# Rearranging the two MLPs of a two-block transformer kernel: when their staging, modulation and last evacuations are issued

## What is computed

```python
def first_block(x, ...):
    for layer in range(2):
        ...                                        # attention of this layer -> mix
        x = layer_norm(ALPHA * x + mix, ...)
        x = layer_norm(ALPHA * x + sqrelu_mlp(x, mlp_w_up[layer], mlp_w_down[layer]), ...)
    return x                                       # sqrelu_mlp: relu(x @ up)**2 @ down, width 4096

def second_block(x, c, ctx, c_ctx, w_ada, ...):
    sh1, sc1, g1, sh2, sc2, g2 = ada(c, w_ada, b_ada)          # silu(c) @ w_ada + b_ada
    csh1, csc1, ... = ada(c_ctx, w_ada, b_ada)
    u_ctx = (layer_norm_2(ctx) * (1 + csc1) + csh1) @ w_in
    u_lat = (layer_norm_2(x) * (1 + sc1) + sh1) @ w_in
    ...                                            # token mixer, post-norm, convolutional FFN
```

## Time and profile before

| what | value |
|---|---|
| time, three runs | 1914.8, 1915.16, 1920.2 us; median 1915.16 |
| the profiled execution | 1919.75 us, of which the span of the trace is 1918.0 us |
| `mlp0`, `mlp1` in the trace | about 317 to 672 us and 946 to 1300 us |
| PE busy | 96% of the span |
| mean granted clock of TensorE | 0.986 of full speed |

### The profile page before, as it was taken

The page is one execution under the profiler, slowest core; times in us unless marked ns, Lnnn a source line. Parts: engine busy times, 40 slices in busy tenths (PEclk is TensorE's granted clock), DMA queues, the critical chain, the costliest instruction groups (busy, mean ns, idle before and its releaser), DMA issues.

```text
span 1918.0 us, 25530 instructions
## 1 busy us (share of the span) xinstructions
PE 1833.0 (96%) x9436; PEld 1491.5 (78%) x9436; DVE 1390.3 (72%) x2217; ACT 883.0 (46%) x1512; POOL 825.0 (43%) x570
## 2 busy tenths in 40 slices
PE   9999899999989999989999998999999999999997
PEld 7876578878777788866887876778887788888876
DVE  4568857888889752175789897985559788676766
ACT  4247643444356432384243444746444554444342
POOL 1234533554541010183345554415346557676740
PEclk9999999999999999999999999999999999999999
DMA  7331032888765432202288877641211323333344
GB/s 282 114 92 45 1 143 92 326 310 298 271 244 189 146 111 93 105 2 88 89 299 314 301 273 271 209 158 67 88 45 66 110 89 110 112 119 121 111 153 153
DMA packets 67048, 297.86 MB, mean 155 GB/s; under 512 B 9008, under 2 KB 9328, under 8 KB 46576
## 3 DMA queue, kind: packets, MB, share of 16 engines
q1 hardware_dynamic: 59872, 254.45, 38.0%
q0 software_dynamic: 7056, 41.80, 5.8%
HBM read 258.54 MB, written 35.65 MB: 153 GB/s over the span
## 4 chain that ended last, share of the span: by engine, by line
PE 65%; DVE 21%; DMA 6%; ACT 3%; issue 2%; POOL 2%; SPq 0%; ACTq 0%; DVEq 0%; POOLq 0%
PE G L474 29%; PE G L2938 8%; PE G L2869 5%; DMA KS_sb<-ada 4%; PE OB L2938 3%; DVE weights_low L685 2%; PE TR L474 2%; PE OB L474 2%; PE G L1923 2%; DVE w_sb L3415 2%; PE TR L2938 2%; PE G L2888 2%; DVE og_sb L3415 2%; PE TR L2869 1%; PE OB L1923 1%
## 5 line engine op out<-in xcount | busy, mean ns | idle before, releaser
L474 PE MATMUL G<-xt_high,weights_high 128*128 128x512 f32 (+1 forms) x1224 | 451.2, 369 | 2.4 <-issue 1.7
L474 PE MATMUL G<-xt_low,weights_high 128*128 128x512 f32 (+1 forms) x1224 | 449.0, 367 | 0.0
L474 PE MATMUL G<-xt_high,weights_low 128*128 128x512 f32 (+1 forms) x1224 | 448.9, 367 | 0.0
L518 POOL TENSOR_TENSOR weights_low<-ring_sb,weights_high 128x1024 fp32r<-128x1024 f32 (+2 forms) x102 | 246.3, 2427 | 285.3 <-ACT weights_high L512 285.3
L512 ACT ACTIVATE weights_high<-ring_sb 128x1024 fp32r<-128x1024 f32 (+2 forms) x188 | 189.8, 1019 | 158.4 <-PE G L2869 40.0
L474 PEld LDWEIGHTS G<-xt_high,weights_high 128*128 128x128 f32 x1224 | 228.7, 187 | 42.6 <-issue 3.7
L474 PEld LDWEIGHTS G<-xt_high,weights_low 128*128 128x128 f32 x1224 | 228.5, 187 | 38.5
L474 PEld LDWEIGHTS G<-xt_low,weights_high 128*128 128x128 f32 x1224 | 228.8, 187 | 37.9
L518 DVE TENSOR_TENSOR weights_low<-ring_sb,weights_high 128x1024 fp32r<-128x1024 f32 (+1 forms) x86 | 109.5, 1282 | 169.3 <-ACT weights_high L512 169.2
L685 DVE TENSOR_TENSOR weights_low<-ring_sb,weights_high 128x1024 fp32r<-128x1024 f32 x130 | 173.3, 1343 | 58.8 <-ACT weights_high L679 58.3
L679 ACT ACTIVATE weights_high<-ring_sb 128x1024 fp32r<-128x1024 f32 x130 | 136.5, 1052 | 73.9 <-PE OB L2938 40.5
(11 more groups left out here) (631 smaller groups left out, 4321.6 us busy)
## 6 DMA issues: line engine op xcount, KB each, us to landing
...
```

The lines of the kernel that those rows point to most:

```text
L474: mm = nc.tensor.matmul(out, lhsT=a, rhs=b, start=(3 * i + j == 0), stop=(3 * i + j == n - 1))
L518: tt_(out=quarter_part(wl, stage, n), in0=quarter_part(raw_quarter(stage, n), stage, n), in1=quarter_part(wh, stage, n), op=ALU.subtract). ...
```

## The change

It has four parts, in both MLPs.

1. **Modulation steps.** The steps run behind c = 1 to 16 and 18 to 26 with no c left out but 17. The sums, the first turn (behind U17 instead of U18) and the copies move up; the second turn stands behind U30 instead of D14.
2. **Staging first.** DVE makes the low part of the staged block, or the hidden sums, ahead of the copy, the move and the modulation steps of the same c. On both ACT and DVE the blocks of D13 and D14 are staged at the start of c = 30 and c = 31, ahead of the weights split there, and the weights of D15 are split after the loop instead of in c = 31.
3. **Eight raw slots in the last phase.** C's raw weights take eight slots, four of them in the first half of `ring`. S15's split weights go to row 0 instead of row 3. The first chunks of the next stage's weights can be loaded once C9 and C11 are split (before, C13 and C15).
4. **Evacuations.** The seventh product is emptied behind S15 instead of behind C1, the sixth behind C4, C5 and C6, the two half statistics of layer norm behind C7. In `mlp1` `scale_columns` goes from behind C3 to behind C8, and the first half of the context's modulation on ACT from C8 to C9.

```diff
+    C_RAW = [(1, 2), (1, 3), (1, 0), (1, 1), (0, 3), (0, 0), (0, 1), (0, 2)]
...
-    ADA_SUM_BEHIND = {7: 0, 10: 1, 13: 2, 16: 3, 21: 4, 25: 5, 28: 6, 31: 7}
-    ADA_TURN_BEHIND = {18: 0}
-    ADA_STEPS = {1: (0, (0,)), 2: (0, (1, 2)), 3: (0, (3, 4, 5)), 4: (0, (6, 7)), 6: (1, (0, 1, 2)), 7: (1, (3, 4, 5)), 8: (1, (6, 7)),
...
-    ADA_COPY, ADA_MOVE = {18: 0}, {20: 0}
+    ADA_SUM_BEHIND = {6: 0, 9: 1, 12: 2, 15: 3, 19: 4, 22: 5, 25: 6, 28: 7}
+    ADA_TURN_BEHIND = {17: 0, 30: 1}
+    ADA_STEPS = {1: (0, (0,)), 2: (0, (1, 2)), 3: (0, (3, 4, 5)), 4: (0, (6, 7)), 5: (1, (0, 1, 2)), 6: (1, (3, 4, 5)), 7: (1, (6, 7))}
+    for job, c in ((2, 8), (3, 11), (4, 14), (5, 18), (6, 21), (7, 24)):
+        ADA_STEPS.update({c: (job, (0, 1, 2)), c + 1: (job, (3, 4, 5)), c + 2: (job, (6, 7))})
+    ADA_COPY, ADA_MOVE = {17: 0, 30: 1}, {18: 0, 31: 1}
...
             if kind == "S":
-                return [x[:, 3, 512 * (u % 2):512 * (u % 2) + 512] for x in (Wh, Wl)]
+                r = 0 if u == UNITS - 1 else 3
+                return [x[:, r, 512 * (u % 2):512 * (u % 2) + 512] for x in (Wh, Wl)]
...
             if kind == "S":
-                return AT[("S", u - 2) if u >= 2 else ("D", 15)] + 1
+                return AT[("B", 15) if u == UNITS - 1 else ("S", u - 2) if u >= 2 else ("D", 15)] + 1
...
                 def last_sums(u):
                     if u < 2:
                         sp.wait_ge(sums_stored[0], down_count(stage, 15))
-                    elif u < 4:
-                        low_made(("B", (15, 13)[u - 2]))
+                    elif u < 5:
+                        low_made(("B", (15, 13, 14)[u - 2]))
+                    elif u < 8:
+                        sp.wait_ge(quarters, q + AT[(("B", 13), ("B", 15), ("S", 15))[u - 5]] + 1)
                     else:
-                        low_made(("C", u - 4))
+                        low_made(("C", u - 8))
...
@@ mlp_scalar (ACT); the loop of mlp (DVE) has the same two moves with block_low and mlp_low
                 for c in range(UPS):
-                    while c and done <= AT["U", c] + 3:
+                    if c == 30:
+                        block_high(act, stage, "0", 13)
+                    elif c == 31:
+                        block_high(act, stage, "0", 14)
+                    while c and done <= min(AT["U", c] + 3, AT["B", 0]):
                         mlp_high(act, stage, *SPLITS[done])
                         done += 1
-                    if c % 2 == 0 and c >= 4:
+                    if c % 2 == 0 and 4 <= c < 30:
                         block_high(act, stage, "0", (c - 4) // 2)
-                    if c == UPS - 1:
-                        block_high(act, stage, "0", 14)
...
+                mlp_high(act, stage, "D", 15)
                 block_high(act, stage, "0", 15)
...
@@ mlp (DVE), inside the loop over c
+                    if c % 2 == 0 and 4 <= c < 30:
+                        block_low(dve, stage, "0", (c - 4) // 2)
+                    elif c % 2 and c >= 5:
+                        hidden_sums(stage, (c - 5) // 2)
                     if c in ADA_COPY:
                         ada_copy(ada + ADA_COPY[c])
                     if c in ADA_MOVE:
                         ada_move(ada + ADA_MOVE[c])
                     if c in ADA_STEPS:
                         ada_steps_of(ada + ADA_STEPS[c][0] // 4, ADA_STEPS[c][0] % 4, ADA_STEPS[c][1])
-                    if c % 2 == 0 and c >= 4:
-                        block_low(dve, stage, "0", (c - 4) // 2)
-                    elif c >= 5:
-                        hidden_sums(stage, (c - 5) // 2)
...
@@ mlp (DVE), behind the weights of each unit
-                    elif (kind, u) == ("C", 1):
+                    elif (kind, u) == ("S", 15):
                         dve.wait_ge(prod_done, ends + 1)
                         dve.wait_ge(dve_out, v + 8)
                         for t in range(2):
                             for half in range(2):
                                 evacuate(2 + t, half, P7B[t])
-                    elif (kind, u) == ("S", 15):
                         quarters_in(dve, stage, AT["B", 15] + 1)
                         dve.wait_ge(dve_out, v + 14)
                         for t in range(2):
                             evacuate(t, 1, P5B[t])
                             evacuate(2 + t, 1, P5B[t])
-                    elif (kind, u) == ("C", 3) and stage == "mlp1":
+                    elif kind == "C" and 4 <= u < 7:
+                        dve.wait_ge(dve_out, v + 18)
+                        quarters_in(dve, stage, AT["S", 15] + 1)
+                        for t in range(2):
+                            evacuate(*((2 + t, 1), (2 + t, 0), (t, 1))[u - 4], P6B[t])
+                    elif (kind, u) == ("C", 7):
+                        early(2, 1, 19)
+                        early(3, 1, 20)
+                    if (kind, u) == ("C", 8) and stage == "mlp1":
                         scale_columns()
```

42 lines of the change are left out of this document (17 added, 25 removed), and 3 rows, old and new, of the table ADA_STEPS.

## The result

| | before | changed |
|---|---|---|
| median (lowest to highest) of 20 runs, us | 1916.03 (1912.88 to 1922.02) | 1906.71 (1902.07 to 1914.05) |
| profiled execution, us | 1919.75 | 1905.22 |
| its span, us; granted clock | 1918.0; 0.986 | 1903.4; 0.989 |

The ratio is 0.995 with an interval of 0.9942 to 0.9959: 0.5% faster, by 9.3 us between the medians and 14.5 us between the profiled pair. The forecast was 34.1 us and a time of 1881, with a range of 1872 to 1894. It missed.

The account below looks back on a forecast made before the run. PE, busy 96% of the span, was taken as the bound, leaving its waits and half clock to win. Net gains of 18.85 us (`mlp0`) and 15.25 (`mlp1`) made 34.1, from a median of 1915.16 to 1881, range 1872 to 1894.

Parts of the forecast that it names:

- The seam's own waits: From U29 to B0: three waits and about 4 us of half clock and restarts go, 12.0 us in `mlp0`.
- the early D waits: The other two D waits in `mlp0`: blocks that stood behind modulation steps now stand ahead, 1.4 us.
- S15 and the third product: Start of the last phase: one wait becomes two, 1.7 and 1.5 us; gain 1.05 us per MLP, bounds 0 and 1.9.
- the C phase: With eight slots C14 no longer waits for loads: gain 1.5 us in `mlp0`, bounds -0.5 and 2.3.
- the norm of `mlp0`: Before the first transposes: the 2.8 us wait and 1.7 us from half clock go, 4.5 us in all.
- The signs named for "wrong": New PE wait over 1 us behind U17, U30 or at B1; wait for L686 in C; U tiles waiting for low parts.
- The turn: PE's turn behind U17 waits for DVE's copy: 0.5 us late, 1.0 for two turns, bounds 0 and 2 each.
- D14 to B6: After U31, DVE's row of work makes B1 0.3 us late and costs 0.3 more: 0.6, bounds 0 and 2.5.
- The norm of `mlp1`: Before the first transposes: a 9.2 us chain against 8.2 us of passes; of 4.1 us wait 1.0 stays, 3.1 go.
- The rule left aside: Sums ahead of a copy can each lose a whole POOL instruction; saving about 4 us smaller, not in the sum.
- the seam turns into new waits: Rival: at each seam a 2.5 us wait plus half clock, 10 us lost in all, 1891; chance 0.20.
- DVE can't keep pace without pauses: Rival: at 3 us more DVE time per pair, 24 us lost an MLP, 1929, slower; chance 0.02.

Follow-up runs that it names:

- `gains_late`: Changed kernel with the norm's gain and bias loads issued behind the eighth block of the B phase instead of ahead of the first; 1903.65 us, ratio 0.9943.
- `best_c`: Changed kernel with first copy behind c = 16, second behind c = 29, gain and bias loads behind the eighth block, unit 15's sums behind B2; 1893.7 us.
- `ctl_late`: Changed kernel with GpSimd's low part of the transposed context in `mlp1` waiting for the end of tile 0's first norm; 1904.49 us, ratio 0.9943.
- `sums15_late`: Changed kernel with unit 15's four hidden sums on DVE moved from ahead of B1's low part to behind B2's; 1902.39 us, ratio 0.9925.
- `pool_narrow`: Changed kernel with GpSimd's four weight sums cut from 512 columns to 8, the rest left out; 1890.57 us, ratio 0.9871.
- `best_b`: Changed kernel: copies behind c = 16 and 29, later gain/bias loads, unit 15's sums behind B6, context behind tile 0's second norm, D15's weights in c = 31; 1898.75 us.
- `best_d`: `best_c` with unit 14's hidden sums moved behind B1 and unit 15's behind B3; 1897.12 us, ratio to the kernel before 0.9904.
- `copy16`: Changed kernel with DVE's first copy of the modulation sums behind c = 16 instead of c = 17; 1897.82 us, ratio 0.9906.
- `sums_narrow`: Changed kernel with DVE's eight hidden sums of units 14 and 15 cut from 256 columns to 8, the rest left out; 1903.11 us, ratio 0.9934.
- `ctl_narrow`: Changed kernel with GpSimd's low part of the transposed context cut to 2 of 256 columns a block, at its old place; 1904.54 us, ratio 0.9943.

## Why the prediction was wrong

**Right.** The seam's own waits (12.0 and 11.7 forecast, 11.5 and 11.3 found), the early D waits, S15 and the third product, which wait 2.1 and 1.3 us and keep the clock, the C phase, and the norm of `mlp0`. That the clock stayed up over both waits at S15 is in part luck: I had counted it as an even chance, and in 8 of the 32 MLPs traced with the new last phase it was at half there (`gains_late` in both, `best_c` in `mlp0`, `ctl_late`, `sums15_late`, `pool_narrow`, `best_b` and `best_d` in `mlp1`). The signs named for "wrong" were those that came: waits over 1 us behind U17 and at B1.

**The turn: the step failed.** It took the time at which DVE reaches the copy from the old trace (428.30), though the change puts five of job 4's steps into c = 15 and 16, just ahead. Nor did it let PE be early by what its own sum gains before: U17 ended at 430.2 (432.87 - 2.66), not at the 432.0 of the old trace. In absolute time the copy came about when forecast, 432.53 to 432.81 against 431.5 or, with one long sum, 432.5; PE was there 1.8 us sooner. Both should have been read from the new order: 2.7 and 3.0 us of wait plus 1.7 of half clock stood where I had put 0.5. `copy16` shows that the place of the copy is the cause. In the traces of the seven kernels that share this place, U17 to D6 took 7.9 to 11.1 us against 5.4. A spread of this size at one place can be behind the changed kernel's wider range (12.0 us, before 9.1), but that isn't shown.

**D14 to B6: mis-sized, 0.6 and the second turn's 0.5 against 5.0 and 5.7.** The chain through DVE to B1 was the right one, but each part was taken at its length when alone: two sums at 1.40 and a block at 1.22 add 2.5 us, and B1's wait is 2.1. Not seen at all was B4's load, which starts when B1's low part is made and came 1.5 us behind 1 MB of gain and bias; it cost PE something in `mlp0` alone. The half clock behind B1 in `mlp1`, 2.8 us, was in no term either. Beneath lies a thing I had not reckoned with, in the second part of the change: D14's block now stands ahead of work that it stood behind. In the kernel before DVE made the weights of B0 and D15 and four sums first, PE waited for it, and B1's block was done (551.04) 7.2 us behind D14's start. In the changed kernel it was done (546.48) 11.1 us behind D14's start, and PE needs it after 8.4. The work that PE no longer waits for at D14 it waits for at B1. How the 5 us divide among DVE's instructions stays partly open: `sums_narrow` takes 2.5 to 2.8 of them, `pool_narrow` 2.1 to 3.7, and the two may overlap.

**The norm of `mlp1`: the step failed.** The chain of 9.2 us was copied from the old trace, where GpSimd's two instructions ran beside evacuations. Moved forward, the norm fell on them: 9.2 + 2.1 = 11.3 us against two passes of 8.2 leaves the 3.2 us found instead of 1.0. `ctl_narrow` gives back 1.1.

**The rule left aside.** I had weighed what the Trainium skill says ("SBUF — State Buffer", section "SBUF: two separate sides") of the lock on a port pair between DVE with two inputs in SBUF and GpSimd, and put about 4 us on it in a sentence outside the sum. With GpSimd's sums narrow the kernel gained 16 us, so it should have stood in the sum. The rule also shows in `ctl_late` at 1275.75: the instruction that comes second waits until GpSimd's has ended, even if it has one element a partition.

Of the rivals, "the seam turns into new waits" was nearest. It gave 1891 at a price of 5 us an MLP; the turn and the stretch D14 to B6 together cost 9.8 and 10.8. That DVE can't keep pace without pauses was there too, but tied to loads late by 3 us a pair and held at 0.02. It came in another form, at c = 14 to 17 alone.
